# Pooling projections ahead of the convolution's in every mixer, and two early prompt rows in other slots

## What is computed

```python
def mixer(h, lp, l, ctx):
    z = h @ lp['w_in']
    zp, zn, zc, zd = ...                    # pooling 512 columns, nat 1536, conv 1024, diff 1536
    y_pool = pool_branch(zp, lp['pool_w'], lp['pool_scale'])   # window mean minus the token itself, then 128x128
    ...
    y_conv = conv_branch(zc, ...)           # a * sigmoid(b), 31 taps per channel, layer norm, silu
    ...                                     # nat: neighbourhood attention; diff: differential attention
    out = merge_branches(h, (y_pool, y_nat, y_conv, y_diff), lp['w_branch'], lp['w_gate'], lp['b_gate'], lp['w_out'])

def peer_ffn(h, ...):                       # per token: 8 heads x 16 experts chosen out of 16384
    act = gelu(einsum(u_tab[e], h)); return einsum(g * act, v_tab[e])
```

## Time and profile before

| | us |
|---|---|
| three runs | 5033.79, 5034.46, 5041.13 |
| median | 5034.46 |
| the profiled execution | 5033.25 |
| its span | 5031.4 |
| busy: PE / DVE / POOL / ACT | 3998.5 / 3378.9 / 1690.2 / 1672.0 |
| expert phase of layer 0 | about 1283 to 2758 |
| latent front of layer 0, of layer 1 | about 324 to 501, 2765 to 2958 |

### The profile page before, as it was taken

How to read it: one execution, slowest core, us unless ns; L and a number is a source line. 1 busy time by engine, 2 the same in 40 slices (tenths; PEclk the granted TensorE clock), 3 DMA queues, 4 the chain that set the end, 5 groups by cost and what they waited for, 6 DMA issues and landing times.

```text
span 5031.4 us, 55082 instructions
## 1 busy us (share of the span) xinstructions
PE 3998.5 (79%) x18548; PEld 1858.9 (37%) x18548; DVE 3378.9 (67%) x7296; ACT 1672.0 (33%) x4905; POOL 1690.2 (34%) x1593
## 2 busy tenths in 40 slices
PE   7999899998777776777766988999887766666676
PEld 4764465446333311344321435644553411111111
DVE  4259766777776786755567566777778767576544
ACT  1211643112333435533333045411223433333333
POOL 3004212221344444433333532222224434444332
PEclk8899999998888888898977999999988976666666
DMA  8843537998999999999998242399979999999998
GB/s 310 294 158 99 181 142 291 361 360 309 366 419 420 414 419 417 402 418 418 419 421 334 79 167 81 132 360 357 348 310 420 420 421 421 421 417 419 421 421 354
DMA packets 277145, 1677.78 MB, mean 333 GB/s; under 512 B 31808, under 2 KB 31856, under 8 KB 112384
## 3 DMA queue, kind: packets, MB, share of 16 engines
q0 software_dynamic: 190896, 1365.43, 66.9%
q1 hardware_dynamic: 82944, 302.03, 16.6%
q10 hardware_dynamic: 3024, 6.82, 0.3%
HBM read 1667.33 MB, written 6.82 MB: 333 GB/s over the span
## 4 chain that ended last, share of the span: by engine, by line
DMA 46%; PE 24%; DVE 16%; issue 5%; ACT 5%; POOL 3%; SPq 0%; DVEq 0%; POOLq 0%; ACTq 0%
DMA arena<-experts,bsb 34%; DMA arena<-experts,peidx 11%; PE ps L1903 5%; PE ps L2336 5%; DVE arena L1795 4%; PE ps L2095 2%; PE ps L2178 2%; PE ps L2200 2%; DVE arena L1463 2%; DVE arena L1583 2%; PE ps L2011 2%; POOL bsb L638 2%; POOL arena L702 1%; PE ps L2217 1%; ACT T L1115 1%
## 5 line engine op out<-in xcount | busy, mean ns | idle before, releaser
L2336 PE MATMUL ps<-arena,T 64*64 64x512 f32 x8192 | 1455.3, 802 | 824.7 <-ACT T L1115 806.6
L1795 DVE CUSTOM_DVE_ANT_0 arena<-arena,h_sb 128x1024 f32<-128x1024 f32 x1024 | 1256.7, 1228 | 915.5 <-DMA arena<-experts,bsb 895.9
L702 POOL DMA_INDIRECT arena<-experts,bsb x1024 | 1109.7, 1084 | 1728.5 <-PE ps L2336 1554.0
L2336 PEld LDWEIGHTS ps<-arena,T 64*64 64x64 f32 x8192 | 265.0, 160 | 1848.9 <-ACT T L1115 1718.3
L1111 ACT ACTIVATE bsb<-T 128x1 f32<-128x1 f32 x1024 | 206.9, 202 | 1537.3 <-DVE T L1795 1519.2
L1903 PE MATMUL ps<-h_sb,wring 128*128 128x256 f32 (+2 forms) x2304 | 545.9, 397 | 26.4 <-DVE h_sb L1547 12.4
L2237 PE MATMUL ps<-h_sb,wring 128*128 128x512 f32 x1024 | 454.4, 597 | 23.9 <-DVE arena L1720 21.5
L1903 PEld LDWEIGHTS ps<-h_sb,wring 128*128 128x128 f32 x2304 | 394.8, 206 | 210.9 <-issue 176.6
L685 POOL DMA_INDIRECT arena<-experts,peidx x224 | 233.0, 1040 | 654.5 <-DVE arena L1463 583.1
L1453 DVE CUSTOM_DVE_ANT_0 arena<-arena,h_sb 128x1024 f32<-128x1024 f32 x256 | 313.0, 1223 | 196.0 <-DMA arena<-experts,peidx 195.1
L1115 ACT ACTIVATE T<-pair,bsb 128x64 f32<-128x64 f32 x1024 | 356.0, 348 | 33.5
(11 more groups left out here) (335 smaller groups left out, 4319.8 us busy)
## 6 DMA issues: line engine op xcount, KB each, us to landing
wring<-w SPq DMA_DIRECT2D x576, 512.0 KB
arena<-experts,bsb POOLq DMA_INDIRECT x1024
bsb<-bias POOLq DMA_DIRECT2D x16, 512.0 KB, 4.0
arena<-subk POOLq DMA_DIRECT2D x4, 1024.0 KB, 8.5
arena<-experts,peidx POOLq DMA_INDIRECT x256, 5.8
arena<-v_scratch POOLq DMA_DIRECT2D x64, 64.0 KB, 2.1
x_sb<-xT POOLq DMA_DIRECT2D x1, 2048.0 KB, 10.0
v_scratch<-arena ACTq DMA_DIRECT2D x8, 256.0 KB, 2.0
```

What stands on the lines that cost most here:

```text
L702: gp.indirect_dma_start(rows[:, n % NS, :], None, experts, bass.IndirectOffsetOnAxis(ap=eidx[:, t % 2, i:i + 1], axis=0)).then_inc(row_in[ ...
L1795: v.tensor_tensor_reduce(e, e, htok(t), 1.0, 0.0, ALU.mult, ALU.add, dots[:, t % 2, i:i + 1]).then_inc(dot, 1)
L2336: mm = pe.matmul(ps[64 * half:64 * half + 64, 6 + g, :], diag[tok, n % ND, :], rows[tok, n % NS, D + half * 512:D + (half + 1) * 512], sta ...
```

## The change

Two edits. The first puts the four pooling projections ahead of the convolution's eight, in the prompt's and in the latent mixers: chunk numbers, host layout, bank turns, and the programs of PE and ACT. `K_POOL` becomes 4, `K_CONV` 8, and the prompt's taps begin with the values' step (`K_TAPS` = `K_DV` = 16 instead of 12). DVE's order in the latent mixers stays. The second reorders the slots of the early rows: row 0 goes to 22144, row 1 to 24704, row 2 to 20096. POOL waits for the first half of the routing before row 0, for the second half before row 1, and for the staged values only before row 2.

```diff
-C_CONV, C_POOL, C_V, C_QK, C_MERGE, C_OUT, C_QUERY, NCH = 0, 8, 12, 20, 36, 84, 92, 108
+C_POOL, C_CONV, C_V, C_QK, C_MERGE, C_OUT, C_QUERY, NCH = 0, 4, 12, 20, 36, 84, 92, 108
...
-K_RMS1, K_CONV, K_POOL, K_DV, K_NV, K_QK = 1, 4, 12, 16, 20, 24
+K_RMS1, K_POOL, K_CONV, K_DV, K_NV, K_QK = 1, 4, 8, 16, 20, 24
...
-K_TAPS, TAPS = K_POOL, 5
+K_TAPS, TAPS = K_DV, 5
...
-        prow0 = [at(arena, a, 2 * D) for a in (20096, 22144, 24704)]
+        prow0 = [at(arena, a, 2 * D) for a in (22144, 24704, 20096)]
...
-                for i in range(2):
-                    gp.wait_ge(vb_out[i], 32 * (l + 1))
                 gp.wait_ge(p_idx, 2 * l + 1)
                 for i in range(EARLY):
+                    if i == 1:
+                        gp.wait_ge(p_idx, 2 * (l + 1))
+                    if i == 2:
+                        for h in range(2):
+                            gp.wait_ge(vb_out[h], 32 * (l + 1))
                     if i >= 3:
                         gp.wait_ge(p_acc, l * PAIRS + i - 2)
...
+                for g in range(4):
+                    wait_unit(act, u(f"pl{g}"))
+                    act.activation(yT[:, g, :], bank(u(f"pl{g}")), ACT.Copy).then_inc(free_of(u(f"pl{g}")), 1)
                 for c in range(4):
                     wait_unit(act, u(f"cb{c}"))
...
-                for g in range(4):
-                    wait_unit(act, u(f"pl{g}"))
-                    act.activation(yT[:, g, :], bank(u(f"pl{g}")), ACT.Copy).then_inc(free_of(u(f"pl{g}")), 1)
...
+                for g in range(4):
+                    project(u(f"pl{g}"), C_POOL + g, 512, h_in if g else h_first)
                 for c in range(4):
-                    project(u(f"cb{c}"), C_CONV + 2 * c, 512, h_in if c else h_first)
+                    project(u(f"cb{c}"), C_CONV + 2 * c, 512, h_in)
                     project(u(f"ca{c}"), C_CONV + 2 * c + 1, 512, h_in)
-                for g in range(4):
-                    project(u(f"pl{g}"), C_POOL + g, 512, h_in)
```

More of the change, by code:

```diff
@@ L159, in latent_units @@
     names = [("rms1", None)] * (l == 0)
+    names += [(f"pl{g}", C_POOL + g) for g in range(4)]
     for c in range(4):
         names += [(f"cb{c}", C_CONV + 2 * c), (f"ca{c}", C_CONV + 2 * c + 1)]
-    names += [(f"pl{g}", C_POOL + g) for g in range(4)]
     for i, b in enumerate(("dv", "nv")):
@@ L735, in prompt_mixer @@
                         act.activation(lam[:, 2:4], lam[:, 0:2], ACT.Exp).then_inc(p_lamexp, 1)
-                    if K_CONV <= k < K_POOL and (k - K_CONV) % 2 == 0:
+                    if K_CONV <= k < K_DV and (k - K_CONV) % 2 == 0:
                         c = (k - K_CONV) // 2
@@ L741, in prompt_mixer @@
                         act.activation(psg[:, c % 2, :], bank(u(f"cb{c}"), P), ACT.Sigmoid).then_inc(free_of(u(f"cb{c}")), 1)
-                    if K_POOL <= k < K_DV:
+                    if K_POOL <= k < K_CONV:
                         name = u(f"pl{k - K_POOL}")
@@ L1311, in prompt_mixer @@
                         own.link(v.tensor_tensor(lam[:, 4:5], lam[:, 4:5], cl[:, 0:1], ALU.subtract))
-                    if K_CONV <= k < K_POOL and (k - K_CONV) % 2:
+                    if K_CONV <= k < K_DV and (k - K_CONV) % 2:
                         c = (k - K_CONV) // 2
@@ L1931, in prompt_mixer @@
                         sums(u("rms1"), P, [psq[:, d, :] for d in range(KD)])
-                    if K_CONV <= k < K_POOL:
-                        if k == K_CONV:
-                            pe.wait_ge(p_h, 2 * l + 1)
+                    if k == K_POOL:
+                        pe.wait_ge(p_h, 2 * l + 1)
+                    if K_CONV <= k < K_DV:
                         c = (k - K_CONV) // 2
                         project(u(f"ca{c}" if (k - K_CONV) % 2 else f"cb{c}"), C_CONV + k - K_CONV, P, h_of)
-                    if K_POOL <= k < K_DV:
+                    if K_POOL <= k < K_CONV:
                         project(u(f"pl{k - K_POOL}"), C_POOL + k - K_POOL, P, h_of)
@@ L2388 @@
         ca, cb = _col_chunks(wi[:, 2048:2560]), _col_chunks(wi[:, 2560:3072])
+        parts.append(_col_chunks(wi[:, 0:512]))
         for c in range(4):
             parts += [cb[c:c + 1], ca[c:c + 1]]
-        parts.append(_col_chunks(wi[:, 0:512]))
         for s in (4096, 1536, 3072, 3584, 512, 1024):
```

## The result

The changed kernel took **5053.77 us** in the median of 20 runs, the kernel before 5037.97 us in 20 runs beside it: a ratio of 1.0032 (95% interval 1.0022 to 1.0042), so some 16 us slower (11 to 21). The forecast was 5048 us, 5039 to 5058, with slower as the likely side. A second set of 12 runs gave 1.0025 (1.0015 to 1.0034), some 13 us. The profiled execution has a span of 5048.9 us against 5031.4, +17.5.

What follows compares the result with a forecast made beforehand. Outside the DMA-saturated stretches engines wait for each other in one chain; layer 0 continues from the end of DVE's taps. Terms +14.6, -1.0, +0.9 and 0 sum to +14.5 us, giving 5048 us, range 5039 to 5058.

Steps and rivals of the forecast that it cites:

- Held products in layer 0: Layer 0's latent mixer: DVE idle 32 us before product 0, fourth product 27.4 us later, taps 13.8 us shorter, ending +13.3 us.
- PE colder behind the gap: Latent fronts: PE's first unit after its gap was taken as 9.4 us, against 7.03 later on.
- the term of +14.6: Layer 0's latent front: second transposes at 515.9 us against 501.3; bounds 13.3 and 19.3.
- the term of -1.0: Layer 1's latent front: 15.69 us wait goes, later taps replace it, third transposes at 2956.8 against 2957.78; bounds -2.4, +4.7.
- Early rows: Earlier gathers of prompt rows: nothing in layer 0; in layer 1 rows 0 and 1 there by 2820, row 2 gives nothing.
- The rule on the port: Layer 0: by the Skill's rule row 1's gather would hold DVE 1.08 us, sum 1.1 us higher; forecast has nothing for it.
- Prompt mixers: Layer 0's prompt mixer: four taps before nk's reciprocal, +0.9 us (0 to +2); layer 1's: 0, bounds -4 to +4.
- The dip of the earlier trace: First expert phase, 2050 to 2100 us: gathers fall to 389 GB/s from 418 behind it, 3.5 us to be had.
- That DVE is not held: Rival, layer 0: pooling projections fit under the routing, product 3 stays at 388.8, -11.7 us in all, 5022; chance 0.07.
- that most comes back: Rival: dip fills (-3.5), layer 1 gains 2.4, the prompt's 0.9 is swallowed; +8.7 us, 5042; chance 0.17.
- the colder PE: Rival, layer 0: PE comes back colder from its gap, +4.7 us, 5052.5; chance 0.12.
- the slots' own worth: Rival: an earlier first row is the gain; true of layer 1 alone, -6 us or so if taps stayed; chance 0.02.

Runs made afterwards that it cites:

- e3: Kernel before with the new order in layer 0's latent mixer only, plus new slots and waits: 5055.15 us against 5035.15, ratio 1.0037.
- e6: Changed kernel with all 144 routing steps of layer 0 ahead of the first latent product: 5042.93 us against 5048.54, ratio 1.0010 to the kernel before.
- e8: Kernel before with only the new slots and waits of the early rows, old projection order: ratio 1.0001.
- e9: Kernel before with new slots, and gathers of rows 0 and 1 ahead of POOL's averages in both layers: 5023.09 us against 5040.42, ratio 0.9966.
- e1: Kernel before run again unchanged: ratio 1.0006.
- e2: Kernel before with the new order in the prompt's mixers only, old slots and waits: 5039.42 us, ratio 1.0008.
- e7: Changed kernel's order in all mixers, with the old slots and waits of the early rows: ratio 1.0018 to the kernel before.
- e12: Kernel before, new slots; layer 0: rows 0 to 2 ahead, averages after taps and between rows; layer 1: rows 0 and 1 ahead of averages. Ratio 0.9965.
- e4: Kernel before with the new order in layer 1's latent mixer only, plus new slots and waits: 5031.92 us, ratio 0.9998.
- e5: Changed kernel run again unchanged in a second set: 5048.54 us, ratio 1.0025 to the kernel before.
- e10: Kernel before, new slots, rows 0 and 1 ahead of averages; in layer 0 also row 2 ahead and averages held until the taps end: ratio 0.9959.
- e11: Kernel before, new slots; both layers: rows 0 to 2 ahead, some averages after the taps, two steps after each further row. Ratio 0.9965.

## Why the prediction was right, point by point

- **Held products in layer 0.** The step was that DVE's first product waits for PE's sixth projection, with the routing behind it: idle 32 us (31.99), the fourth product 27.4 us later against the first latent matmul (26.7), the averages over near 365, 41 us behind that matmul (357.0, or 39 us behind it in an execution that reaches it 6 us sooner), 120 taps in 79.59 us (79.59). The taps' end was to move by 13.3 us and moved by 12.5; the difference is in the last stretch of routing, which I had taken from the earlier trace rows as 19.7 us. It ended there beside POOL's first copy, and no longer does. The last routing instruction, before and after:

```profile
387.87 0.99 DVE L1255 CAST peidx<-arena 128x64 uint32<-128x64 f32 x1
```

```profile
409.22 0.20 DVE L1258 CAST peidx<-arena 128x64 uint32<-128x64 f32 x1
```

  e3 has this idle time and this delay by itself, e6 shows the mechanism.
- **PE colder behind the gap.** I took 9.4 us for the first unit; it took 8.91. With this the term of +14.6 measured **+13.0**. In layer 1 the unit took 8.44, and the term of -1.0 measured **-2.2** at the third transposes and -1.3 at the first scores. Direction and place were right, this one duration was too long: I had tied it to the gap's length by two rows of one execution, and more rows do not bear that out (last section).
- **Early rows.** Nothing in layer 0, and in layer 1 only through the averages: e8 confirms that the slots alone do nothing. That in layer 1 the later taps take the place of the wait was the forecast, and e9 shows what the wait was worth without them, 13.6 us.
- **The rule on the port.** Row 1's gather ran from 410.19 to 411.28 us, and the first tap began at 411.99, so no tap met it: whether a gather already begun holds a tap, the 1.1 us that my sum left out, was not put to the test. The four instructions that it did meet read one 128x512 input each, and were not held up (1.92 us, 1.91 in e9's layer 1 with POOL idle). The Trainium skill, page "SBUF — State Buffer", section "Who interferes with whom", has a VectorE instruction with two SBUF inputs and a GpSimd instruction that reads SBUF exclude each other for one instruction. The traces disagree on the length: 75.14 us for a copy, 30.57 and 22.60 us for gathers, beside running taps of 0.66 us.
- **Prompt mixers.** +0.9 forecast, +0.6 measured for nk's transposes of layer 0. For layer 1's, the expert phase of layer 0 differs by 0.3 us. The dip of the earlier trace rows stays, though these fixed windows say little: the phase begins 20.7 us later in this execution, and in e1, e2 and e3 the first window has 390, 363 and 368 GB/s. Windows of POOL in the changed kernel, 2050 to 2100 and behind it:

```profile
2050.00:2100.00 50.00, 22.68 (x19) 0.77 0.99 379
2100.00:2150.00 50.00, 23.11 (x19) 0.90 1.01 416
```

- **Rivals.** That DVE is not held fell with the first row; that most comes back fell with the front's 13 us and with the dip that stays; the colder PE fell with 8.91 us; the slots' own worth fell with e7 and e8. The chances for these and the forecast add up to 0.98, not to 1.
- **Size.** The located terms are +13.4 (first scores of layer 0), -1.3 and +0.6, together 12.7 us, for a forecast of 14.5 and times of 16 (11 to 21) and 13 (8 to 17). One term is missing from the sum: attention and merge of layer 0. In the five executions with the new order in layer 0 they took 534.9 to 539.5 us together, 537.7 on average, in the six others with the old front 530.1 to 535.7, 532.3 on average. That is some 5 us more; the two groups barely overlap, but no run ties it to the change, and the prediction had nothing for it. With it the sum would be 18 us. So the mechanism of the front was right, and that the total came so close is in part luck: the located terms were forecast 1.8 us too high, and the missing 5 us point the other way. The profiled pair's +17.5 holds some 9 us more in these two stages and 6 us less ahead of the first latent matmul; the latter is of the kind that the last section describes. The range, too, is narrower than the terms: their bounds, added one to one, give +6.9 to +29.0 us, so 5040 to 5062, where the prediction has 5042 to 5056.

## What to carry to other kernels

Before moving a producer later in one engine's order, look at what its consumer's engine has programmed behind the wait: here 48 us of independent routing were held behind one product, for 32 us, and placing them ahead gave back 9 of 13 us. When a transfer is late, follow its queue upwards to the first instruction that cannot start; here it was a copy shut out for 75 us, and issuing two gathers ahead of it brought 17 us, where the reordering of the matmuls cost 13 to 16. A wait that is removed is worth only what does not take its place: without the 15.7 us wait, but with the taps 27.4 us later, layer 1 gained 1 us, and with the taps where they were 13.6. And follow a gain to the end of the next stages: the 5.4 us of e12's front in layer 0 were gone at the end of its merge, in the one execution with a trace.

## What the runs showed of the hardware

- **A train of taps on DVE shuts POOL out as a whole, unless POOL is already at work.** A copy or a gather that came into a running train stood until its end, in nine places: copies for 75.14 (before and e8) and 75.13 us (e9), gathers for 30.57 and 22.60 (changed kernel), 21.95 (e6), 21.74 (e7), 18.45 (e9) and 18.06 us (before), where they take 0.61 and 0.94 to 1.09 us otherwise. Where POOL's averages had begun ahead of the train (layer 0 in the kernel before and in e9) both went on in turn and the 120 taps took 93.49 and 93.86 us instead of 79.6.
- **The first unit behind a gap of PE** took 8.28, 8.03, 8.44, 8.78, 9.41 and 8.91 us after gaps of 9.97, 13.79, 13.80, 13.80, 14.15 and 22.39 us (the kernel before, e6, after, e4, before, after), and 7.03 us in e9 without such a gap. With nearly the same gap it took 8.85, 8.86 and 9.27 us (e3, e5, e7: 22.39, 22.37, 22.43 us). The granted clock over that unit was 0.82 in layer 1 of the changed kernel, where 8.44 us were taken, and 0.74 over the 9.41; the gap's length alone does not set it.
- **Stretches with the same program differ between executions.** The first latent matmul of layer 0 stood between 315.3 and 325.7 us, early or late with either order in the prompt's mixer (317.1 in e4 and 324.2 in the kernel before with the old, 318.1 in the changed kernel and 323.6 in e2 with the new). Attention of layer 0, whose program is the same in all fourteen executions, took 184.4 to 192.6 us. Sorted by the granted clock of its first 60 us: 184.4 to 186.8 us at 0.89 (before, e1, e8, e9), 187.1 to 189.8 at 0.86 (e2, e6, e10), 190.0 and 190.8 at 0.83 (e11, e3), 187.9 to 188.4 at 0.80 (after, e4, e5, e7) and 192.6 at 0.77 (e12). The highest clock goes with the shortest attention, but below it the order breaks. All five executions with the new order in layer 0 are below 0.89, and so are e2 and e4, whose front of layer 0 has the old order. What decides this clock, and so whether the change costs something behind its front, stays open.
